# Expert weights read as one 16 KB run per partition, with the token rows and the hidden units in the matching order

## The reference, cut to what matters

```python
DEPTH, D_MODEL, D_EXPERT, N_EXPERTS, TOP_K = 2, 1024, 512, 32, 2
# w_expert_in [DEPTH, 32, 1024, 1024], w_expert_out [DEPTH, 32, 512, 1024]
order = jnp.argsort(flat_e)                    # the 1024 (token, expert) pairs, sorted by expert
xs = t[tok_s]                                  # their token rows
hu = lax.ragged_dot(xs, w1, sizes)             # [1024 pairs, 1024]: gate and up
h_gate, h_up = jnp.split(hu, 2, axis=-1)
ys = lax.ragged_dot(jax.nn.silu(h_gate) * h_up, w2, sizes)
ys = ys * flat_gate[order][:, None]
out = jnp.zeros_like(t).at[tok_s].add(ys)
```

## Time and profile before

| | |
|---|---|
| time, median of 3 runs | 3999.5 us (3993.81 to 3999.94) |
| the profiled execution's own time | 4006.49 us |
| its span | 4004.8 us |
| TensorE matmuls busy | 3338.8 us, 83% of the span |
| VectorE, ScalarE, GpSimd busy | 30%, 21%, 17% |
| read from HBM | 655.47 MB, of which expert weights 198 transfers of 2048 KB |
| the ring's transfers from issue to landing, median | w_expert_in 23.7 us, w_expert_out 24.8 us |

### The profile page before, as it was taken

How to read it: one execution, slowest core, us unless ns; L and a number is a source line. 1 busy time by engine, 2 the same in 40 slices (tenths; PEclk the granted TensorE clock), 3 DMA queues, 4 the chain that set the end, 5 groups by cost and what they waited for, 6 DMA issues and landing times. The chain is left out here.

```text
span 4004.8 us, 41122 instructions
## 1 busy us (share of the span) xinstructions
PE 3338.8 (83%) x14329; PEld 1956.9 (49%) x14329; DVE 1182.0 (30%) x2139; ACT 858.7 (21%) x1253; POOL 671.3 (17%) x367
## 2 busy tenths in 40 slices
PE   5796798788884796698788786788799988879999
PEld 3573364433332574364433332553488447338854
DVE  2356402211112347511211110363333015433310
ACT  0523211111111423311111111222232022323300
POOL 2311010111111221010111111300234021013300
PEclk7897898899997897799799999888899999889999
DMA  8311023799997421023699999210132322012222
GB/s 300 120 52 41 11 90 122 312 409 409 409 406 288 162 73 36 5 95 128 236 397 408 410 409 364 73 43 1 63 99 65 90 87 84 1 42 85 92 65 64
DMA packets 287753, 665.18 MB, mean 166 GB/s; under 512 B 20282, under 2 KB 110704, under 8 KB 287600
## 3 DMA queue, kind: packets, MB, share of 16 engines
q1 hardware_dynamic: 269632, 623.43, 41.8%
q0 software_dynamic: 17968, 39.73, 2.8%
HBM read 655.47 MB, written 25.44 MB: 170 GB/s over the span
## 5 line engine op out<-in xcount | busy, mean ns | idle before, releaser
L822 PE MATMUL psum<-s_parts 128*128 128x512 f32 (+3 forms) x3392 | 830.3, 398 | 112.3 <-ACT s_parts L1908 96.6
L822 PE MATMUL psum<-s_ring,s_units 128*64 128x512 f32 x3168 | 746.2, 621 | 128.7 <-DMA s_ring<-in_w_expert_in 89.9
L822 PEld LDWEIGHTS psum<-s_parts 128*128 128x128 f32 (+1 forms) x3392 | 637.6, 194 | 277.0 <-issue 99.9
L822 PEld LDWEIGHTS psum<-s_ring,s_units 128*64 128x64 f32 x3168 | 250.7, 142 | 580.8 <-issue 450.9
L822 PE MATMUL psum<-s_units,s_ring 128*128 128x512 f32 x1216 | 524.0, 593 | 3.3 <-DVE s_units L1581 3.3
L822 PE MATMUL psum<-s_units 128*128 (+9 forms) x1532 | 406.0, 450 | 128.1 <-ACT s_units L1908 52.5
L801 POOL TENSOR_TENSOR s_parts<-s_ring,s_parts 128x4096 fp32r<-128x4096 f32 x30 | 270.1, 9008 | 996.5 <-ACT s_parts L1908 996.5
L822 PEld LDWEIGHTS psum<-s_units,s_ring 128*128 128x128 f32 x1216 | 231.2, 190 | 290.5 <-issue 289.7
L822 PE MATMUL psum<-s_h_low,s_parts 128*128 128x512 f32 (+1 forms) x1440 | 355.9, 389 | 0.0
L822 PEld LDWEIGHTS psum<-s_units 64*128 64x128 f32 (+3 forms) x1532 | 206.7, 206 | 258.2 <-issue 198.2
L822 PEld LDWEIGHTS psum<-s_h_low,s_parts 128*128 128x128 f32 (+1 forms) x1440 | 269.1, 187 | 57.5
(11 more groups left out here) (313 smaller groups left out, 2425.2 us busy)
## 6 DMA issues: line engine op xcount, KB each, us to landing
s_ring<-in_w_expert_in SPq DMA_DIRECT2D x132, 2048.0 KB, 23.7
s_ring<-in_w_expert_out SPq DMA_DIRECT2D x66, 2048.0 KB, 24.8
s_ring<-in_w_in SPq DMA_DIRECT2D x28, 2048.0 KB, 7.9
s_ring<-in_w_ada SPq DMA_DIRECT2D x24, 2048.0 KB, 19.7
s_ring<-in_ffn_w_up SPq DMA_DIRECT2D x44, 1024.0 KB, 6.7
s_ring<-in_ffn_w_down SPq DMA_DIRECT2D x16, 1408.0 KB, 7.7
s_ring<-in_w_out SPq DMA_DIRECT2D x8, 2048.0 KB, 7.8
s_units<-ys_scratch POOLq DMA_DIRECT2D x16, 512.0 KB, 6.3
```

The costliest lines, as they stand in the source:

```text
L822: return pe.matmul(o, lhsT=lhsT, rhs=rhs, start=start, stop=stop)
```

## The change

It loads the same bytes into the same slots, with another feature on each partition. Feature 8 p + k of the input, and hidden unit 4 p + k of the output weights, now lie on partition p, so that a partition's 16 KB are one run in memory. In `w_expert_in`, the run of half j is half of the partition's 32 KB. To match, the token-major copy writes feature 8 p + r to place 128 r + p of the row: its innermost step in the destination is 128 elements. In `gate_up` the columns of a matmul are taken so that hidden unit 4 q + 2 c + i comes out at place 128 i + q of half c: the moving operand is read with a step of 4 elements (16 bytes) over q, where it was read in runs of 256. Numbers of instructions, sizes and waits are the same.

```diff
@@ -544,9 +544,10 @@
                 sp.wait_ge(freed_in_m[j].sem, freed_in_m[j].at(number, u - 1))
                 settle(sp)
                 if j < 2:
-                    sp.dma_start(slot_view(s, 4, D), kn(inp["w_expert_in"][l, e], 0, D)[:, 4 * j:4 * j + 4, :]).then_inc(weights_in_m[s], 16)
+                    rows = inp["w_expert_in"][l, e].rearrange("(p k) n -> p (k n)", p=P)[:, SLOT * j:SLOT * j + SLOT]
                 else:
-                    sp.dma_start(slot_view(s, 4, D), kn(inp["w_expert_out"][l, e], 0, D)).then_inc(weights_in_m[s], 16)
+                    rows = inp["w_expert_out"][l, e].rearrange("(p k) n -> p (k n)", p=P)
+                sp.dma_start(ring[:, s, :], rows).then_inc(weights_in_m[s], 16)
@@ -1150,8 +1151,8 @@
                     for k in range(4):
                         for c in range(2):
                             half = slice(CAP * c, CAP * c + CAP)
-                            both = w[:, k, :].rearrange("p (h f) -> p h f", h=2)[:, :, 256 * c:256 * c + 256]
-                            last = mm(psum[half, u, :].rearrange("p (h f) -> p h f", h=2), xsT[u][:, k, CAP * j:CAP * j + CAP],
+                            both = w[:, k, :].rearrange("p (h q c i) -> p c h i q", h=2, c=2, i=2)[:, c]
+                            last = mm(psum[half, u, :].rearrange("p (h i q) -> p h i q", h=2, i=2), xsT[u][:, k, CAP * j:CAP * j + CAP],
                                       both, j == 0 and k == 0, j == 1 and k == 3)
@@ -2081,7 +2082,8 @@
-                copy(h2t[(i // 2) % 2][:, 512 * (i % 2):512 * (i % 2) + 512], o).then_inc(TA.by(("tm", i)).sem, TA.by(("tm", i)).more())
+                turned = h2t[(i // 2) % 2].rearrange("s (r k b) -> s k b r", r=8, k=KD)[:, 4 * (i % 2):4 * (i % 2) + 4]
+                copy(turned, o.rearrange("s (k b r) -> s k b r", k=4, r=8)).then_inc(TA.by(("tm", i)).sem, TA.by(("tm", i)).more())
```

## The result

The changed kernel takes 4349.0 us (median of 4 runs, 4343.9 to 4356.6), the kernel before beside it 3996.7. The ratio is 1.088, with a 95% interval from 1.086 to 1.091: slower by 352 us, where the forecast had 281 and a range that ended at 4330. The profiled executions took 4352.1 and 4006.5 us.

The account below looks back on a forecast made before the run. It took DMA as the late units' bound, with TensorE becoming the bound after the change: 279 us from slower gate_up plus 2 for copies, 281 on 4006.5, giving 4287, or 4280 on the median's scale; range 3950 to 4330.

Parts of the forecast that it names:

- The bound before: Experts' units before the change: DMA sets the late pace, 16.29 us per unit, with two other limits close behind.
- the scatter's loop: Experts' units: the ring of scatter, landing and down limits early units to 13.88 us each.
- The third limit: TensorE's own work in an experts' unit before the change: 13.88 - 0.9 = 12.98 us.
- The moving operand: gate_up's 16-byte-step read slows its passes: 6.9 us more per unit, bounds from nothing to 7.5.
- the sum for TensorE's time per unit: Experts' units after the change: 12.98 + 6.9 = 19.9 us, making TensorE the bound instead of 15.76 us per unit.
- I take a doubling, 6.9 us: gate_up's stepped passes take twice as long, adding 6.9 us per unit, between estimates of 5.8 and 7.5.
- the clock stays at 1.00: A sign of being right: TensorE stays at 2.4 GHz in the units, as it rests less.
- the two first `gate_up`: First unit of each layer: one more slowed gate_up each, 2 x 6.9 = 14 us.
- The packets: Weight transfers: 16 KB packets take 615 ns in place of 642, saving 0.65 us per unit, at most 40 us.
- The token-major copies: Eight copies a layer, each 0.36 us longer from 512-byte write steps; mostly covered, 2 us in all.
- The faster rival: Experts' units: the stepped read is free and larger packets are cheaper, giving 3960 us; chance 0.25.
- The scatter rival: Experts' units: steps free, but 16 KB packets delay each scatter by up to 3.6 us, giving 4111 us; chance 0.13.

Follow-up runs that it names:

- g3: The kernel before with only VectorE's read of bank 7 made early, taking the scatter's landing off TensorE's path: 3993.7 us, ratio 0.999.
- e3: The changed kernel with gate_up reading two hidden units of a pair together (8 bytes in a run, 16-byte step), activations' transposes stepped instead: 4053.9 us, ratio 1.014.
- g1: e3 plus VectorE's early read of bank 7, which takes the scatter's landing off TensorE's path: 3954.7 us, ratio 0.989.
- e1: The changed kernel with gate_up's moving operand read in runs of 256 columns again (output differs, 64 units instead of 66): 4024.5 us, ratio 1.007.

## Why the prediction was right or wrong

**The bound before** was read rightly: DMA in the late units (g3 gains nothing to speak of without the loop), the scatter's loop close behind it (e3 and g1 differ by it). The third limit, TensorE's own work, was read too low: 13.88 - 0.9 = 12.98, where g3 shows 13.3.

**The moving operand** was the right mechanism with too low a price. The step that failed is the sum for TensorE's time per unit, 12.98 + 6.9 = 19.9 us, where the intervals measured 21.22. Three of its parts were too small.

- "I take a doubling, 6.9 us": a pair of passes measured 0.90 us, which is the prediction's upper bound, 1.75 ns per element from the reduce of the earlier trace rows, to within 1%. The rows had the price; the value taken lay between it and another one. It makes 16 x 0.47 = 7.5 us per unit, 38 us over the 64 intervals.
- TensorE's own work of 12.98 us. Taking the 0.9 us wait for `s_gsl` off 13.88 left out the wait for the activations that stood hidden behind it. g3's 12.7 and 13.85 us plus 7.5 are the 20.2 and 21.4 us of the changed kernel's undisturbed units, 20.8 on average and not 20.5: some 20 us.
- The prediction had that "the clock stays at 1.00". In 14 of the 64 intervals it falls, at the start of `down` or up to 3 us earlier, which takes the mean from 20.8 to 21.2: some 27 us. In 900 to 1200 us the mean clock is 0.97, as before.

The price of the step alone would not have been enough: with 7.5 us the prediction's sum gives 4318 us, and 4349 was measured. With all three, 281 becomes 366, 14 above the measured 352. That rest lies outside the intervals, where the sum had 16 us for the two first `gate_up` and the copies and 3 us came back. One piece of it is in the rows: the first `gate_up` of layer 1 ran at the lower clock already before, so that it grew only from 9.1 to 14.7 us, 5.6 us. The other pieces are open.

**The packets** were as forecast: 16 KB each, and in g1 a stream of 423 GB/s where 4 KB rows gave 408. 642 / 615 ns is a factor of 1.044, measured 1.037.

**The token-major copies** take 1065 ns in place of 594, 0.47 us more and not 0.36, and cost nothing: from the first copy to the first gather it is 15.49 us before (705.62 to 721.11) and 15.55 after (703.07 to 718.62).

**The faster rival** was wrong as I gave it. With a nearly free read of the operand (e3) the kernel is slower than before by 1.4%. Its 3960 needs the landing off the path too; then it is 3955 (g1).

**The scatter rival** was right in its place, and hidden here as forecast: no wait for `s_gsl` remains in the changed kernel. The price per packet was too high (3.6 us by turns, measured 1.4), so a scatter's rows don't wait for a whole 16 KB packet each. But its deciding point, a landing of 8.1 us, was too late: at 7.5 us the kernel already loses, because the lower clock adds 1.7 us that no term had. How these two share the loss is read from the rows, not tried one by one; g1 removed both together.

**The Trainium skill** (SBUF — State Buffer, section Door 1: The DMA port swizzle): its first half, full speed from two hits per 16-byte line, agrees with 0.45 us at two elements per line and 0.90 at one. Its half on how far one may step for free does not hold at four fp32: that step costs in full.

## What to carry to other kernels

A layout that suits the DMA is paid for where the data is read: before a matmul's moving operand is stepped, count the 16-byte lines it touches; here 1.76 ns for each was the pace of fp32 passes, at either clock, and two elements per line were almost free (other types were not measured). A stream's gain shows only if nothing else stands just behind it: list the loops that stand within some 15% of the bound (here 13.88 us behind 16.29), and ask for each what larger packets do to small transfers in it. And a pause of TensorE can cost its length twice, through the clock of the work behind it.

## What the runs showed that I had not expected

- The prices on VectorE and TensorE came out alike: 1.75 ns per element, an estimate from one reduce in steps of 32 bytes, and 1.76 ns per column in fp32 passes with 16-byte steps.
- Two passes side by side on TensorE, each with its own stepped operand, run no slower than that; a stepped pass alone was not run. The DMA's writes add nothing: 0.90 us with 4 KB packets, with 16 KB packets and with the DMA engines idle. Nor does the clock: 0.90 us at 1.00 and at 0.50.
- Packets four times as large delay a scatter by 1.4 us (6.1 to 7.5) in e1 and e3, where the DMA share is 0.95, by 1.9 (8.0) in g1, where it is 1.00, and by only 0.3 (6.3 to 6.6) where TensorE holds the stream back to 0.82. So the delay needs a nearly full stream beside the large packets; its mechanism was not tried.
- After a wait of some 2.4 us in which TensorE did nothing, with short transposes and other small matmuls around it, the next matmuls ran at the lower clock (e1: four steps of 0.85 us). After a wait of 0.9 us they did so in some units only (the changed kernel).
